# A pair loop whose transposes become products, whose 128-wide products become halves, and whose last turn gets other work to fill it

## The reference

```python
def step(S, inp):
    rt, wt, kt, vt, at, bt = inp
    sa = jnp.einsum('bhij,bhj->bhi', S, at)
    S = S * wt[:, :, None, :] + sa[..., None] * bt[:, :, None, :] + vt[..., None] * kt[:, :, None, :]
    return S, jnp.einsum('bhij,bhj->bhi', S, rt)
```

## Time and profile before

| | |
|---|---|
| median of 3 runs | 1989.6 us (1989.52 to 1990.25) |
| the profiled execution: its time, its span | 1990.38 us, 1988.8 us |
| TensorE busy over the span | 1807.5 us, 91% |
| VectorE, ScalarE, GpSimd busy | 526.8, 316.1, 335.1 us |
| mean granted TensorE clock, as a share of full speed | 0.955 |
| transfers | 573.89 MB, mean 289 GB/s |
| the eight pairs | 265.2 to 797.5 us |
| the product with `w_out` and what lies around it | 807.8 to 955 us |
| router and experts | from there to the end |

### The profile page before, as it was taken

The page is one execution under the profiler, slowest core; times in us unless marked ns, Lnnn a source line. Parts: engine busy times, 40 slices in busy tenths (PEclk is TensorE's granted clock), DMA queues, the critical chain, the costliest instruction groups (busy, mean ns, idle before and its releaser), DMA issues. The chain is left out here.

```text
span 1988.8 us, 27906 instructions
## 1 busy us (share of the span) xinstructions
PE 1807.5 (91%) x11069; PEld 940.2 (47%) x11069; DVE 526.8 (26%) x1232; ACT 316.1 (16%) x674; POOL 335.1 (17%) x489
## 2 busy tenths in 40 slices
PE   5669999999999987899878999999999999999996
PEld 2137655555555544677424444353543435344352
DVE  2152244355445544010321121101112011111203
ACT  2001123123213321100501101001110101110102
POOL 0020012112211210100000040301304021130303
PEclk8679999999999998899779999999999999999998
DMA  8994357455745544664129999999999999999993
GB/s 282 335 330 112 91 159 239 145 194 162 237 142 198 162 145 115 170 209 150 43 118 428 428 427 428 429 427 428 419 428 429 429 428 423 429 428 428 429 423 116
DMA packets 191109, 573.89 MB, mean 289 GB/s; under 512 B 10691, under 2 KB 114461, under 8 KB 165363
## 3 DMA queue, kind: packets, MB, share of 16 engines
q1 hardware_dynamic: 187230, 563.76, 73.5%
q0 software_dynamic: 3200, 6.20, 1.3%
q10 hardware_dynamic: 631, 3.27, 0.6%
HBM read 567.78 MB, written 5.65 MB: 288 GB/s over the span
## 5 line engine op out<-in xcount | busy, mean ns | idle before, releaser
L1768 PE MATMUL PS<-ring,xt 128*64 128x512 f32 x2048 | 493.7, 605 | 27.1 <-DMA ring<-in_w_up 25.6
L1768 PEld LDWEIGHTS PS<-ring,xt 128*64 128x64 f32 x2048 | 196.6, 138 | 290.3 <-issue 244.1
L1975 POOL TENSOR_TENSOR x<-x,tmp 128x512 f32<-128x512 f32 (+1 forms) x96 | 125.2, 1308 | 669.4 <-DVE tmp L1892 669.4
L1801 PE MATMUL PS<-ring,att 128*64 128x512 f32 x1024 | 227.5, 593 | 0.0
L699 PE MATMUL PS<-ring 128*64 128x320 f32 x1344 | 212.9, 439 | 0.0
L1801 PEld LDWEIGHTS PS<-ring,att 128*64 128x64 f32 x1024 | 116.8, 137 | 95.6 <-issue 58.3
L1892 DVE TENSOR_TENSOR tmp<-PS,catT 128x512 f32<-128x512 f32 (+1 forms) x96 | 66.1, 689 | 300.1 <-PE PS L1755 296.0
L364 PE MATMUL PS<-ring,silT 128*32 128x512 f32 x768 | 110.1, 700 | 34.6 <-DMA ring<-in_w_ada 32.1
L1420 PE MATMUL PS<-catT,ring 128*128 128x320 f32 x512 | 138.7, 433 | 0.0
L1903 DVE TENSOR_TENSOR sgt<-sgt,PS 64x1024 f32<-64x1024 f32 x16 | 19.4, 1213 | 426.4 <-ACT sgt L1831 426.4
L1736 PE MATMUL PS<-h,pick 128*64 128x512 f32 x408 | 108.6, 606 | 10.0 <-DVE pick L1873 10.0
(11 more groups left out here) (411 smaller groups left out, 1671.2 us busy)
## 6 DMA issues: line engine op xcount, KB each, us to landing
ring<-in_w_gate SPq DMA_DIRECT2D x64, 2048.0 KB, 12.5
ring<-in_w_up SPq DMA_DIRECT2D x64, 2048.0 KB, 16.1
ring<-in_w_down SPq DMA_DIRECT2D x64, 2048.0 KB, 15.9
ring<-in_w_ada SPq DMA_DIRECT2D x48, 2048.0 KB, 8.8
ring<-in_w_in SPq DMA_DIRECT2D x34, 1024.0 KB, 5.7
ring<-in_w_out SPq DMA_DIRECT2D x16, 1024.0 KB, 5.9
x_a<-in_x_prompt ACTq DMA_DIRECT2D x2, 1024.0 KB, 8.3
sraw<-in_state_wkv POOLq DMA_DIRECT2D x8, 256.0 KB, 3.7
```

The lines of the kernel that those rows point to most:

```text
L1768: m = nc.tensor.matmul(PS[C * g:C * g + C, c, :], xt[:, 4 * q + k, :], unit(2 * q + g, FE)[:, k, 512 * c:512 * c + 512], start=(q == 0 and ...
L1801: m = nc.tensor.matmul(PS[C * (c % 2):C * (c % 2) + C, 4 + c // 2, :], att[:, 2 * q + k, :], unit(u, D)[:, k, 512 * c:512 * c + 512], star ...
L1975: nc.gpsimd.tensor_tensor(xx, xx, tmp[0:n_, r % 2, :], ALU.add).then_inc(x_ok, 1)
```

## The change

In `phase_b` alone, but for one piece of `phase_mix`:

1. **Levels.** `turned` and `spread` go. A level now is `each(3)`, two units, two ScalarE copies of 64 partitions into a block-diagonal tile `zbd`, `each(2)` as before, and a new `each(0)` with the operands exchanged, which gives the transposed update at once; VectorE writes it into `invt` under a transposed mask `lvl_t[:, n]` (two masked writes). The fifth level has only the transposed product. One unit follows.
2. **Halves.** The low-rank products, the sum of squares, the bonus product, mean and variance, and the block products of L801 are issued as two halves of 64 columns (`wide`, and a loop over `half`).
3. **Order.** `norm(i)` moves from the head of the next pair to the end of its own; `cse` becomes `cx`, in `ka`'s place, after `k2`, and no longer waits for `fin`; all of `bk` is formed on VectorE; the bonus product moves to the last step of the block loop, into `W[2]`; `first` and the `zlast` copies move into level 3; `ada` and `turn` take other places (the second chunk before level 1 and before the block loop); the ScalarE table for sigmoid is loaded at the end of the pair before.
4. **Fill of the last pair.** In pair 7, `fill` issues 15 of the 16 k-tiles of `product(0, j)` for j = 1, 0, 2 (45 units, `mixed`), and `phase_mix` adds the last k-tile of these three. SyncE therefore issues the first `w_out` transfers ahead of the last modulation chunk's.
5. **Shift rows.** 16 transposes, a copy, 11 transposes, a copy, all in banks 3 to 6.

```diff
-F_PREP, F_TOK, F_MM, F_LEVEL, F_G, F_U, F_ST, F_SCAN, F_END = 11, 3, 3, 1, 1, 1, 1, 4, 2
-N_DVE, N_POOL = 41, 10
+F_PREP, F_VT, F_TOK, F_Z, F_E, F_G, F_U, F_ST, F_Y, F_SCAN, F_END = 8, 2, 3, 2, 1, 1, 1, 1, 1, 4, 2
+N_DVE, N_POOL = 42, 8
...
+            def mixed(j, k, i):
+
+                if k == 0:
+                    pe.wait_ge(G["s_wo"][j], 16)
+                    pe.wait_ge(z_done, i + 1)
+                elif k == KT - 2:
+                    pe.wait_ge(fin, i)
+                for r in half:
+                    nc.tensor.matmul(PS[r, j, 0:T], G["wo"][:, j, k, r], catT[:, k, :], start=(k == 0), stop=False,
+                                     skip_group_check=True)
...
+            def wide(bank, left, right, start=True, stop=True):
+
+                for r in half:
+                    m = nc.tensor.matmul(W[bank][r, 0:T], left[:, r], right, start=start, stop=stop,
+                                         skip_group_check=True)
+                return m
...
-                units = iter([] if last else [(j, k) for j in (1, 0, 2) for k in range(KT)])
+                units = iter([(j, k) for j in (1, 0, 2) for k in range(KT - 1)] if last else
+                             [(j, k) for j in (1, 0, 2) for k in range(KT)])
...
                 for n in range(1, LEVELS + 1):
-                    pe.wait_ge(inv_ok, 6 * i + n)
+                    pe.wait_ge(inv_ok, 5 * i + n)
                     if n == 1:
                         pe.wait_ge(abd_ok, i + 1)
-                    else:
-                        pe.wait_ge(mm_ev, i + 1)
-                        turned()
                     each(3, lambda c, h: abd[:, c, h, :], lambda c, h: inv[:, c, :], True, True).then_inc(t_z, 1)
-                    if n == 1:
-                        fill(F_LEVEL)
-                    elif n == 2:
-                        turn(i, 0)
-                    elif n <= 4:
-                        ada(i, 1, n - 3)
+                    fill(F_Z)
                     pe.wait_ge(z_cp, 5 * i + n)
                     pe.wait_ge(bd_ok, 6 * i + n)
                     if n == 1:
                         pe.wait_ge(mm2_ev, i + 1)
-                    each(2, lambda c, h: invt[:, c, h, :], lambda c, h: zs[:, c, :], True, True).then_inc(t_e, 1)
-                    fill(F_LEVEL)
-
-                pe.wait_ge(inv_ok, 6 * i + 6)
-                turned()
+                    if n < LEVELS:
+                        each(2, lambda c, h: invt[:, c, h, :], lambda c, h: zbd[:, c, h, :], True, True).then_inc(t_e, 1)
+                    if n == 1:
+                        pe.wait_ge(mm0_ev, i + 1)
+                    each(0, lambda c, h: zbd[:, c, h, :], lambda c, h: invt[:, c, h, :], True, True).then_inc(t_et, 1)
+                    fill(F_E)
...
                 for n in range(1, LEVELS + 1):
                     act.wait_ge(t_z, 6 * i + n + 1)
-                    nc.scalar.copy(zs[:, :, :].rearrange("p c t -> p (c t)"), W[3][:, 0:T]).then_inc(z_cp, 1)
-                    if n in (1, 4):
-                        a_copy(n // 4)
+                    for h, r in enumerate(half):
+                        m = nc.scalar.copy(zbd[r, :, h, :], cut(W[3][r, 0:T]))
+                    m.then_inc(z_cp, 1)
...
                 for n in range(1, LEVELS + 1):
-                    if n >= 2:
-                        spread(n - 1)
-                    ve.wait_ge(t_e, 5 * i + n)
-                    put(inv[:, :, :], lvl_n[:, n, :], cut(W[2][:, 0:T])).then_inc(inv_ok, 1)
-                    if n == 2:
-                        ada_store(i, 0, o, last)
-                spread(5)
+                    if n < LEVELS:
+                        ve.wait_ge(t_e, 4 * i + n)
+                        put(inv[:, :, :], lvl_n[:, n, :], cut(W[2][:, 0:T])).then_inc(inv_ok, 1)
+                    ve.wait_ge(t_et, 5 * i + n)
+                    for h, r in enumerate(half):
+                        m = put(invt[r, :, h, :], lvl_t[r, n, :], cut(W[0][r, 0:T]))
+                        if h == 0:
+                            o.did(m)
+                    m.then_inc(bd_ok, 1)
...
-                if not isinstance(i, int) or i:
-                    norm(i - 1)
-                ve.wait_ge(k2_ok, i + 1)
-                nc.vector.scalar_tensor_tensor(out=rk[:, :], in0=zr[:, :], scalar=pc[:, K_RK:K_RK + 1], in1=k2[:, :],
-                                               op0=ALU.mult, op1=ALU.mult).then_inc(rk_ok, 1)
...
-                for k in range(KT):
+                if isinstance(g, int) and g == 0 and j < 3:
+                    for h in range(2):
+                        r = slice(64 * h, 64 * h + 64)
+                        m = nc.tensor.matmul(PS[r, j, 0:T], wo[:, j, KT - 1, r], catT[:, KT - 1, :], start=False,
+                                             stop=True, skip_group_check=True)
+                for k in () if isinstance(g, int) and g == 0 and j < 3 else range(KT):
                     m = nc.tensor.matmul(PS[:, j, 0:T], wo[:, j, k, :], catT[:, k, :], start=(k == 0),
                                          stop=(k == KT - 1))
                 m.then_inc(u_wo, 1)
```

More of the change, by code:

```diff
@@ L570, in _ @@
                                      ).then_inc(ld_a2[u], 16)
+            for j in (1, 0, 2, 3):
+                if j < 3:
+                    sp.wait_ge(wu[j], UBASE[j] + PAIRS)
+                sp.dma_start(G["wo"][:, j], G["w_out"][:, :, j * P:(j + 1) * P]).then_inc(G["s_wo"][j], 16)
             for u in range(2):
@@ L573, in _ @@
                 sp.dma_start(abuf[:, u], w_ada[u, :, :, 23 * 512:24 * 512]).then_inc(ld_a2[u], 16)
[L575 to L579, removed]
+            sp.wait_ge(sh_ev, 2)
             for dst, r0, nr in (("shift_p", 0, 1), ("shift_s", 1, NB)):
@@ L645, in pair @@
                 o.settle()
-                pool.wait_ge(z_done, i + 1)
+                pool.wait_ge(sq_ok, i + 1)
                 nc.gpsimd.tensor_tensor(k2[:, :], zk[:, :], ka[:, :], ALU.mult).then_inc(k2_ok, 1)
                 pool.wait_ge(k2_ok, i + 1)
[L649 to L654, removed]
+                pool.wait_ge(cs_ok, i + 1)
+                nc.gpsimd.tensor_tensor(cx[:, :], cs[:, :], sg[:, :], ALU.subtract).then_inc(cse_ok, 1)
                 if not last:
@@ L963, in pair @@
             def pair(i, last):
+                earlier(act, zl_ok, i)
                 for j in (1, 0, 2):
@@ L984, in pair @@
                 nc.scalar.preload_act_table_set("natural_log_exp_and_others")
+                act.wait_ge(l_g, i + 1)
+                earlier(act, fin, i)
+                nc.scalar.copy(gg[:, :], W[3][:, 0:T]).then_inc(lev, 1)
                 act.wait_ge(ssm_ok, i + 1)
@@ L1093, in _, with first @@
                 ve.sem_inc(lzs_ok, 1)
+            def first(i, o):
+                for j in range(3):
+                    zc = z3[:, j, 1 + NP_TOK:ZW].rearrange("p (b l) -> p b l", l=ZS)
+                    o.did(nc.vector.tensor_copy(zc[:, :, 0].unsqueeze(1), sprevT[:, at(i + 8 * j), :]))
+            first(0, o)
+            o.settle()
             base = o.n
@@ L1189, in pair @@
                 for h, r in enumerate(half):
-                    m = put(invt[r, :, h, :], lvl_t[r, :], abd[r, :, h, :])
+                    m = put(invt[r, :, h, :], lvl_t[r, 0, :], abd[r, :, h, :])
                     if h == 0:
```

214 lines of the change are left out of this document (109 added, 105 removed).

## The result

The changed kernel takes 1957.4 us (median of 4 runs, 1954.0 to 1963.8) against 1989.9 for the one before: a ratio of 0.984, 95% interval 0.981 to 0.987. The forecast was 1924, in a range from 1909 to 1946. The sign was right and half the gain is missing: 32 us came off where 65.6 were forecast.

A forecast was written before the change was run, and what follows sets the result against it. TensorE, busy but not packed, bounds the kernel. Gains of 46.1 us (seven pairs), 5.0 (last pair and block end) and 14.5 (output products), 65.6 off 1990.38, gave 1924.8, taken as 1924; range 1909 to 1946.

The forecast's parts named there:

- A pair, summed: Steady pair: 66.89 us less waits 5.4, level work 1.1 and halves 0.5, taken as 60.2; seven pairs gain 46.1 us.
- (a): Rival, chance 0.22: inside a pair a chain, not TensorE, sets the time; a pair is 62.7 us, total 1944.
- (c): Rival, chance 0.05: VectorE and GpSimd collide on their shared port in the fill, 8 x 0.9 us more, total 1931.
- (d): Rival, chance 0.03: a level runs in series at 5.4 us, 40 levels add 72 us, total 1996, slower than before.
- (e): Rival, chance 0.02: halves and waits cancel, and only the output products' wait remains; total about 1989 us.
- F2: Theory from the experiments, not the forecast: the loop body's place across 256-instruction fetch blocks decides whether it is fetched again.
- The levels: Inside a pair: 1.1 us less TensorE work; a level takes 3.6 us, set by TensorE, its waits gone.
- The head: Start of a pair: waits for `rk`, `bk` and `bv` gone, 0.5 us a pair kept as the bound.
- Halves: 128-wide products in a pair issued as halves save tiling-mode changes, 0.5 us a pair; block products 2.2 against 2.4.
- Last pair and block end: Last pair 58.45 us to the state transposes, then 11.6 to the next block: 70.05 for 75.07, gain 5.0.
- The output products: 45 k-tiles leave, 24.5 us; less 7.7 waiting for `w_out`, 2 at half clock, 0.3 slow start: gain 14.5.
- (b): Rival, chance 0.1: the output products don't wait for `w_out`; 9.7 us come back, total 1914.

The follow-up runs named there:

- run 11: Changed kernel, loop kept, block products whole, SyncE's first three `w_out` parts asked for ahead of the first expert load: 1918.5 us, ratio 0.963.
- run 15: Kernel before with 40 small redundant products a pair and 224 semaphore increments ahead of TensorE's first product: a loop turn took 70.0 us.
- run 6: Changed kernel with 256 semaphore increments ahead of TensorE's first product: 1991.8 us (one run).
- run 8: Changed kernel with only its block products issued whole again: 1932.0 us.
- runs 4 and 7: Kernel before, each pair lengthened on TensorE: by 160 semaphore increments, 2163.4 us; by 40 small redundant products, 2007.2 us.
- run 5: Changed kernel with 128 semaphore increments ahead of TensorE's first product: 1935.1 us (one run).
- run 12: Kernel before with only its eight 128-wide products and five block products a pair issued as halves, nothing reordered: 1998.5 us (one run).
- run 10: Changed kernel, TensorE's pair loop written out, SyncE's first three `w_out` parts asked for ahead of the first expert load: 1918.0 us, ratio 0.962.

## Why the prediction came out wrong

**The step that failed** is "A pair, summed", where it says "I take 60.2. Seven pairs: 467.48 - 421.4 = 46.1 us gained". It counts TensorE's work and its waits for other engines, and multiplies by seven. Five of those pairs are reached by a jump back, and the step has no term for what the jump costs when the body has grown by 152 instructions. None of the five rivals had it, nor did the range: 39.9 us. Rivals (a), (c), (d) and (e) laid a slow pair on chains and ports inside it; all of the loss was between two pairs. No view of the kernel before shows the loss, since its steady turns fetch nothing; what could have been seen is the size of the body, 1450 records growing to 1602, and, in the q8 line, that instructions come by transfer at all.

**What the cause is.** Shown: the pauses come with instructions fetched again. Of the runs that keep the loop, those with pauses in every turn have 80 or 81 packets, the one with a pause in one turn 44, and all others 33 to 36. They go when the loop is written out, when the body is 20 instructions shorter (but for one turn in run 11), or when the same body is shifted by 24 to 128 instructions; they return at 256. The jump's own record shows it as well (count, then ns least, median and most, where the least is the exit from the loop; before, in the changed kernel, in run 15):

```profile
L920 PEldq COMPARE_BRANCH  x6: 76/208/237, 392.7 to 729.4; - x6
L928 PEldq COMPARE_BRANCH  x6: 83/3846/3944, 383.7 to 724.0; - x6
L926 PEldq COMPARE_BRANCH  x6: 83/3768/3994, 427.2 to 778.0; - x6
```

The block edges can be read too. In the changed kernel TensorE's sequencer issues three records behind the jump, of which this is the last, and nothing more until 392.27:

```profile
L778 PEldq FUSED_REGOPS  x1: 44/44/44, 387.8 to 387.8; - x1
```

That is a second wait, of 4.2 to 4.7 us. It stands behind the third record in all five turns, and again in run 6 (4.1 to 4.7). In run 11, with 20 records fewer ahead of the loop, it stands behind the 23rd; in run 15, with 227 more (counted in the traces), behind the 32nd, which is what blocks of 256 want. Laid out from this edge, the bodies of the changed kernel and of runs 6 and 15 touch eight blocks and reach 42 to 63 records into the last; those of runs 8 and 11 reach 23 into it and are fetched again in one turn of ten; and all other loops touch seven, also those of runs 4 and 7, which are as long as run 15's but begin at an edge. So F2 holds, and 24 instructions were enough because the edge lies three behind the head. Open: why eight touched blocks are too many.

What sets the length of a pause is seen in the same records. The jump waits 3.5 to 4.0 us in either order, and TensorE has 3.0 us (changed order) or 3.5 us (run 15) of work left to cover it. Then comes the wait at the edge: right behind the head in the changed order, where nothing covers it, and 32 records later in run 15, ahead of waits that would have come anyway.

**The levels: right.** 3.55 us against 3.6, no idle; the cover of 0.1 us that ScalarE had was enough: two copies took 0.85 us (0.8 forecast). **The head: right**, no waits for `rk`, `bk` or `bv`. Rival (a), a chain that sets the pair, had no case.

**Halves: mis-sized.** Whole against halves in the new order is 60.9 against 59.5 in unlike loops, and 60.9 against 59.95 in like ones: 0.95 us a pair, against 0.5. All of it is in the eight wide products; the block products gave nothing (pairs of 59.94 us with them whole in run 8, 59.95 with them halved in run 5), where 0.2 was forecast. In the old order all of them together gave 0.4 (run 12, one trace). So the halves earned 7 x 0.95 = 6.7 us here and, by their place, cost 39.9.

**Last pair and block end: better than forecast**, 67.4 against 70.05: the state transposes start 57.1 us into the pair (58.45 forecast), and the rest takes 10.4 (11.6). **The output products: right**, 13.8 against 14.5, with the wait at its size and in its place; rival (b) falls in the changed kernel, and run 10 shows that its case can be made by the order of the queue. **The shared port: harmless.** `kk` now takes 0.49 us, and the product behind it 1.04 beside GpSimd's `ka`, but with halves no pair without a pause is over 60.2 us.

With the loop written out the median is 1923.3 for a forecast of 1924, and part of that is luck. In its trace seven pairs gain 50.5 us (46.1 forecast), the last pair 7.6 (5.0) and the output products 15.2 (14.5), 7.7 us more than forecast in all; a first pair that starts 11.8 us late takes that back, and the experts return 1.7. So the terms were near, each on the cautious side, and one was missing.

## What to carry to other kernels

Before a loop body grows, read the page's line for transfers of instructions and count the body: if packets appear in steady turns, the body is fetched again and the jump back may cost, and an edit elsewhere in the program can bring or remove it by moving the body. Look at the jump's own record (0.2 us when nothing is fetched, 3.5 to 4.7 when something is), at the first instructions after it for idle time with the releaser "issue", and at their duration for half clock. Judge such an edit with its loop written out beside it, or at two places: one run at one place can be off by 2% for a reason that has nothing to do with the edit.

## What the runs showed of the hardware that wasn't expected

A loop body of the same instructions cost 59.95 or 67.9 us a turn by its place alone, and a shift of 24 instructions decided. A jump back whose target had to be fetched took 3.5 to 4.7 us, against 0.2, and the next block edge 4.1 to 4.7 us more when it lay 3 records behind the head. A semaphore increment on TensorE's queue took about 0.136 us (an idle of 21.78 us for 160), while 20 matrix passes of 64 columns start within 0.6 us. And the time to the first pair differs by up to 12 us between runs in which nothing ahead of it differs (267.3, 279.8; with the transfer rate from 30 to 60 us at 281 and 261 GB/s), so stages are compared from their own start.
